# Expert layers of a flow step in passes of 32 slots a head, experts ranked by their count of tokens

## The reference

```python
g_prob = softmax(x @ w_rg + b_rg)                       # 4 groups
g_p, g_i = top_k(g_prob, 1)
e_logits = (x @ w_re + b_re).reshape(-1, 4, 8)
e_v, e_i = top_k(e_logits of group g_i, 2)
gate = softmax(e_v) * g_p
combine = sum(one_hot(g_i * 8 + e_i, 32) * gate)
hid = silu(einsum('nd,edf->nef', x, w_g)) * einsum('nd,edf->nef', x, w_u)
hid = hid * combine
y = hid.reshape(n, 32 * 256) @ w_d.reshape(32 * 256, 1024)
```

## Time and profile before

| | |
|---|---|
| median of 3 runs | 1045.17 us (1044.41 to 1047.46) |
| profiled execution | 1044.07 us |
| its span in the profile | 1042.0 us |
| PE busy | 923.9 us (89%) |
| DVE / ACT / POOL busy | 461.0 / 226.1 / 100.4 us |
| gate and up, L1008 | 229.6 us busy |
| down, L1027 | 116.9 us busy |
| combine, L994 and L995 | 78.6 and 75.6 us busy |
| moved by DMA | 303.99 MB, mean 292 GB/s |
| queue of the weights | 277.08 MB |

### The profile page before, as it was taken

The page is one execution under the profiler, slowest core; times in us unless marked ns, Lnnn a source line. Parts: engine busy times, 40 slices in busy tenths (PEclk is TensorE's granted clock), DMA queues, the critical chain, the costliest instruction groups (busy, mean ns, idle before and its releaser), DMA issues.

```text
span 1042.0 us, 11903 instructions
## 1 busy us (share of the span) xinstructions
PE 923.9 (89%) x4136; PEld 462.2 (44%) x4136; DVE 461.0 (44%) x1037; ACT 226.1 (22%) x458; POOL 100.4 (10%) x164
## 2 busy tenths in 40 slices
PE   2699999999799999999988997899589999999970
PEld 0355454645344444444433465445434444444430
DVE  1257632244323543543555474624515435435454
ACT  2223132212211112112122115212122121111121
POOL 2300011300210000000001000020100000000000
PEclk9899999998799999999998999999689999999995
DMA  9992350948899999999998523021699999999911
GB/s 301 361 351 81 132 184 18 363 167 303 341 398 419 421 420 420 419 422 420 407 372 299 178 81 131 0 87 41 259 418 419 421 420 420 421 420 420 401 50 60
DMA packets 76423, 303.99 MB, mean 292 GB/s; under 512 B 9784, under 2 KB 10096, under 8 KB 50920
## 3 DMA queue, kind: packets, MB, share of 16 engines
q1 hardware_dynamic: 66072, 277.08, 67.2%
q0 software_dynamic: 9040, 21.77, 5.9%
q10 hardware_dynamic: 1280, 4.72, 1.2%
HBM read 310.80 MB, written 5.32 MB: 303 GB/s over the span
## 4 chain that ended last, share of the span: by engine, by line
PE 70%; DMA 14%; DVE 7%; issue 3%; ACT 3%; SPq 2%; POOL 0%; POOLq 0%; DVEq 0%; ACTq 0%
PE psum L1008 18%; PE psum L692 16%; PE psum L1027 8%; DMA ring<-in_w_exp_up 7%; PE psum L764 4%; PE psum L890 4%; PE psum L716 3%; PE psum L980 3%; DVE ht L1767 3%; DMA arena<-h_rows,arena 3%; DMA ring<-in_w_in_odd 2%; DMA ring<-in_w_mod 2%; PE psum L938 1%; PE psum L1131 1%; PE psum L788 1%
## 5 line engine op out<-in xcount | busy, mean ns | idle before, releaser
L1008 PE MATMUL psum<-ring,arena 128*64 128x512 f32 x1024 | 229.6, 601 | 7.4 <-DMA ring<-in_w_exp_up 3.8
L692 PE MATMUL psum<-ring,ht 128*128 128x512 f32 (+1 forms) x432 | 171.9, 555 | 3.4 <-ACT ht L1199 2.7
L1008 PEld LDWEIGHTS psum<-ring,arena 128*64 128x64 f32 x1024 | 82.9, 139 | 151.3 <-issue 151.0
L1027 PE MATMUL psum<-ring,arena 128*64 128x512 f32 x512 | 116.9, 598 | 8.8 <-DVE ht L1767 7.1
L692 PEld LDWEIGHTS psum<-ring,ht 128*128 128x128 f32 x432 | 81.9, 192 | 86.2 <-issue 78.2
L1767 DVE TENSOR_TENSOR ht<-ht,psum 128x512 f32<-128x512 f32 x180 | 110.6, 681 | 4.1 <-PE psum L995 2.2
L1811 DVE TENSOR_TENSOR arena<-arena,psum 128x256 f32<-128x256 f32 x32 | 13.5, 421 | 186.0 <-ACT arena L1342 186.0
L1798 DVE SCALAR_TENSOR_TENSOR y_low<-psum,arena,y_top 128x512 fp32r<-128x512 f32 x64 | 48.0, 751 | 83.6 <-ACT y_top L1349 83.6
L1349 ACT ACTIVATE y_top<-psum,arena 128x512 fp32r<-128x512 f32 x64 | 44.0, 687 | 181.7 <-PE psum L1027 181.7
L994 PE MATMUL psum<-y_top,to_token 128*128 128x512 f32 x192 | 78.6, 409 | 3.5 <-DVE y_low L1798 3.5
L995 PE MATMUL psum<-y_low,to_token 128*128 128x512 f32 x192 | 75.6, 394 | 0.0
(11 more groups left out here) (292 smaller groups left out, 869.4 us busy)
## 6 DMA issues: line engine op xcount, KB each, us to landing
ring<-in_w_exp_gate SPq DMA_DIRECT2D x32, 2048.0 KB, 18.0
ring<-in_w_exp_up SPq DMA_DIRECT2D x32, 2048.0 KB, 22.9
ring<-in_w_exp_down SPq DMA_DIRECT2D x32, 2048.0 KB, 20.5
ring<-in_w_mod SPq DMA_DIRECT2D x24, 2048.0 KB, 18.2
ring<-in_w_in_even SPq DMA_DIRECT2D x5, 2048.0 KB, 19.9
shift_scale<-mod_rows POOLq DMA_DIRECT2D x3, 2048.0 KB, 11.3
ring<-in_w_in_odd SPq DMA_DIRECT2D x3, 2048.0 KB, 21.2
ring<-in_w_out_even SPq DMA_DIRECT2D x2, 2048.0 KB, 8.5
```

Source lines behind the costliest of these rows:

```text
L692: mm = pe.matmul(psum[:, to, 0:cols], HT[:, b, k, :], w[:, k, :], start=(k == 0), stop=(k == KC - 1))
L1008: mm = pe.matmul(psum[64 * e:64 * e + 64, 2, :], XT[:, k, 64 * e:64 * e + 64], RG[:, 3 * v:3 * v + 2, e, k, :], start=(k == 0), stop=(k == ...
L1027: mm = pe.matmul(psum[64 * e:64 * e + 64, 4 + n, :], HTS[v][:, k, 64 * e:64 * e + 64], RD[:, 3 * v + 2, e, k, n * 512:(n + 1) * 512], star ...
```

## The change

1. **Slots.** An expert has 32 slots in a pass (`SLOTS`) instead of 64 in a pair. The array is used in four column groups: gate and up of both experts at once, for which 32 products of 256 columns replace 16 of 512. The down product is cut in the same way: both experts and both halves of the 1024 channels, 8 products of 512 columns in four groups. The result of a pass is one bank: rows 0 to 63 the channels' first half, rows 64 to 127 the second.
2. **Passes.** A round has 22 passes: six heavy places (pairs of experts) with two passes each, then ten light ones with one. An expert of a light place may have 32 tokens, one of a heavy place 64, before a second round is needed.
3. **Rank.** DVE ranks the 32 experts by their count of tokens, the first four experts ahead of all others, since their weights are loaded before the ranks are known. It makes the rank of each token's expert and from this its place; an array `order` gives SP the expert of each rank. SP reads two numbers of it a pair and loads each expert by itself (1 MB a load). A slot is given back by ACT (`gate_up_used`, `down_used`) after the last pass of a pair.
4. **Combine.** Twelve products as before, each over 64 rows only, alternating between rows 0 to 63 and 64 to 127; `to_token` holds the slots twice, so the places' product is made twice. The twelve stand in two parts, before and behind the transposes of `hidden`.
5. **No passes ahead of the loop.** The loop holds all 22 passes; the first one combines zeros. `ACC` is cleared by POOL (a memset of `ht`, 3072 columns) instead of being written by the first pair. Where a semaphore would have been waited for at a value of zero or less, it starts higher.
6. Semaphores of the ring are shared (`first_in_`, `second_in_`).

The core of the diff:

```diff
-HALF = 64
-MAX_ROUNDS = T // HALF
+SLOTS = 32
+HEAVY, LIGHT = 6, 10
+PASSES = 2 * HEAVY + LIGHT
+MAX_ROUNDS = T // (2 * SLOTS)
...
-PLACES = MAX_ROUNDS * PAIRS + 4
+PLACES = MAX_ROUNDS * PASSES + 4
...
+BACK_BANKS = (6, 3, 1, 7, 5, 6)
...
+            def load_experts(l, a, of_pair, slot):
...
+                for e in range(2):
+                    sp.dma_start(RS[:, slot, e:e + 1], w[:, bass.ds(of_pair[e], 1), :]).then_inc(S(f"{('first', 'second')[l]}_in_{slot}"), 16)
...
                 R = rounds_of(sp, l)
+                sp.wait_ge(S("rounds_ready"), 2 * l + 2)
...
+                        place = sp.snap(((i * 2 + u) % PAIRS) * 2)
+                        of_pair = [sp.value_load(order[0:1, bass.ds(place + e, 1)].bitcast(U32), min_val=0, max_val=N_EXP - 1) for e in range(2)]
...
+                        sp.wait_ge(S(f"moe{l}_gate_up_used"), used)
...
+                pool.wait_ge(S("routing_ps"), 4 * l + 1)
+                pool.memset(ht_t[:, :], 0.0).then_inc(S("rows_cleared"), 1)
...
                 pe.wait_ge(S("routing_sb"), 3 * l + 3)
                 for i in range(6):
-                    mm = pe.matmul(psum[:, 7, 0:2 * PLACES], in_slot[:, i, :], in_pair[:, i], start=(i == 0), stop=(i == 5))
+                    for side in range(2):
+                        rows = slice(2 * SLOTS * side, 2 * SLOTS * (side + 1))
+                        mm = pe.matmul(psum[rows, 7, 0:2 * PLACES], in_slot[:, i, :], in_pair[:, i], start=(i == 0), stop=(i == 5))
...
+                def turn_rows(q, v):
+
+                    pe.wait_ge(M(f"gathered_{v}"), (q - v) * 8 + 16)
+                    pe.sem_inc(S("pe_waited"), 1)
+                    for k in range(KC):
+                        t = pe.transpose(psum[:, 0, 2 * SLOTS * k:2 * SLOTS * (k + 1)], XS[v][:, k:D:KC], ident[0:2 * SLOTS, 0:2 * SLOTS])
+                    t.then_inc(M("x_ps"), 1)
+
+                def combine(q, v, blocks):
+
+                    for b in blocks:
+                        for part, rows in enumerate((Y_HI, Y_LO)):
+                            for n in range(2):
+                                if b == NB - 1 and part == 0 and n == 1:
+                                    pe.wait_ge(M("added"), q * 6 + 13)
+                                side = slice(2 * SLOTS * n, 2 * SLOTS * (n + 1))
+                                mm = pe.matmul(bank(BACK_BANKS[2 * b + n]), to_token[v][side, b * P:(b + 1) * P], rows[side, :], start=(part == 0), stop=(part == 1))
...
+                def one_pass(r, p):
+
+                    q = r * PASSES + p
+                    v = p % 2
+                    heavy = p < 2 * HEAVY
+                    place = p // 2 if heavy else p - HEAVY
+                    u = place % 2
+                    new_weights = not heavy or p % 2 == 0
...
                     for k in range(KC):
-                        for e in range(2):
-                            mm = pe.matmul(psum[64 * e:64 * e + 64, 2, :], XT[:, k, 64 * e:64 * e + 64], RG[:, 3 * v:3 * v + 2, e, k, :],
-                                           start=(k == 0), stop=(k == KC - 1))
+                        for a in range(2):
+                            for e in range(2):
+                                to = 2 * SLOTS * (1 - a) + SLOTS * e
+                                mm = pe.matmul(psum[to:to + SLOTS, 2, 0:256], XT[:, k, SLOTS * e:SLOTS * (e + 1)], RG[:, 3 * u + a, e, k, :],
+                                               start=(k == 0), stop=(k == KC - 1))
                     mm.then_inc(M("gate_up"), 1)
+                    turn_rows(q + 1, 1 - v)
+                    if p == 0:
+                        pe.wait_ge(S("table_ready"), 2 * l + 2)
+                        pe.wait_ge(S("rows_cleared"), 7 * l + 7)
+                    results_of(q - 1)
+                    combine(q - 1, 1 - v, range(0, 2))
+                    pe.wait_ge(M("hidden"), q + 3)
...
+                    combine(q - 1, 1 - v, range(2, 3))
+                    pe.wait_ge(M("hidden_t"), q + 1)
...
+                link(dve.scalar_tensor_tensor(key, total, 32.0, key_add, ALU.mult, ALU.add))
...
+                link(dve.tensor_tensor(against, key_other, key_of, ALU.is_gt))
+                link(dve.tensor_reduce(rank, against, AX.X, ALU.add))
...
+                link(dve.tensor_tensor(against, ranked, places_, ALU.is_equal))
+                link(dve.tensor_tensor(against, against, experts_, ALU.mult))
+                link(dve.tensor_reduce(key, against, AX.X, ALU.add))
+                dve.tensor_copy(order.bitcast(U32), key).then_inc(S("rounds_ready"), 1)
```

More of the change, by code:

```diff
@@ L176, in fills_of, with landed_sem @@
 def fills_of(j):
-    return sum(slot_of(i) == slot_of(j) for i in range(j + 1))
+    start = 0 if j < len(FIRST) else len(FIRST)
+    return sum(slot_of(i) == slot_of(j) for i in range(start, j + 1))
+def landed_sem(j):
+    return f"{'first' if j < len(FIRST) else 'second'}_in_{slot_of(j)}"
 def last_in(slot, upto):
@@ L1031, in landed @@
-                def landed(q, v):
-                    return (q - v) * 8 + 16
-                turn_rows(0, 0, first=True)
-                pair(0, 0, first=True)
-                pair(1, 1)
-                R = rounds_of(pe, l)
-                with pe.Fori(1, R * (PAIRS // 2)) as i:
-                    for v in range(2):
-                        pair(i * 2 + v, v)
-                combine(R * PAIRS - 1, 1)
-            experts(0)
+                    if new_weights:
+                        weights_in(2)
@@ new lines, in experts @@
+                start_ = l * len(FIRST)
+                landed = [16 * sum(slot_of(start_ + j) == slot for j in range(len(part_))) for slot in range(RING)]
+                pe.sem_inc(M("back_ps"), 6)
+                pe.sem_inc(M("hidden_ps"), 2)
+                pe.sem_inc(M("down"), 2)
+                pe.wait_ge(S("rest_row_ready"), mods(f"norm_{u}")[0] - FRONT + 1)
+                turn_rows(0, 0)
+                R = rounds_of(pe, l)
+                with pe.Fori(0, R) as r:
+                    for p in range(PASSES):
+                        one_pass(r, p)
@@ L1047, in _ @@
+                last = R * PASSES - 1
+                results_of(last)
+                combine(last, 1, range(0, NB))
+                return last
+            last = experts(0)
             gate, gain = mods("norm_2")
             mod_products(gate)
+            pe.wait_ge(S("moe0_added"), last * 6 + 14)
             mod_sum(gate)
@@ L1354, in experts @@
+                act.sem_inc(M("y_top"), 2)
+                x_copy(0)
                 R = rounds_of(act, l)
-                with act.Fori(1, R * (PAIRS // 2)) as i:
-                    for v in range(2):
-                        pair(i * 2 + v, v)
+                with act.Fori(0, R) as r:
+                    for p in range(PASSES):
+                        one_pass(r, p)
             experts(0)
@@ L1800, in pair @@
[L1800 to L1807 removed]
+                        a = dve.tensor_scalar(to_token[v][:, b * P:(b + 1) * P], iota[:, 0:P], float(b * P), token[v][:, 0:1],
+                                              ALU.add, ALU.is_equal)
@@ L1815, in hidden @@
[L1815 to L1824 removed]
+                    dve.tensor_tensor(HID[v], SGM[v], psum[0:2 * SLOTS, 2, 0:256], ALU.mult).then_inc(M("hidden"), 1)
@@ new lines, in experts @@
+                dve.wait_ge(S("table_ready"), 2 * l + 2)
+                dve.wait_ge(S("rows_cleared"), 7 * (l + 1))
+                dve.sem_inc(M("hidden"), 2)
+                dve.sem_inc(M("y_low"), 2)
+                dve.sem_inc(M("to_token"), 1)
+                dve.sem_inc(M("added"), 6)
+                R = rounds_of(dve, l)
+                with dve.Fori(0, R) as r:
+                    for p in range(PASSES):
+                        one_pass(r, p)
+                last = R * PASSES - 1
```

357 lines of the change are left out of this document (178 added, 179 removed).

## The result

| | before | changed |
|---|---|---|
| median of the runs | 1046.32 us (1044.41 to 1048.54, 4 runs) | **1091.8 us** (1091.36 to 1092.0, 4 runs) |
| span of the profiled execution | 1042.0 | 1089.2 |
| weights' rate, 400 to 500 us | 420 GB/s | 396 GB/s |
| light (before: any) pair in the stream | 15.54 us | 16.64 us |

The change makes the kernel 4.2% slower: ratio 1.042, 95% interval 1.0396 to 1.0444. Forecast were 1067 us and a range of 1044 to 1096.

A forecast was written before the change was run, and what follows sets the result against it. The weight stream was taken to bound the expert layers, PE only 0.5 us a pair behind. Span 1042.0 + 18.3 (layer 1) + 4.1 (layer 2) = 1064.4, giving a forecast of 1067 us, range 1044 to 1096.

The forecast's parts named there:

- A pass: PE in the expert layers: one pass sums to 8.5 us, a light pair taking one and a heavy pair two.
- Short passes: Rival: expert-layer passes take 7.75 us or less but routing delays the stream's start; 1051 us, 20% chance.
- Long passes: Rival: combine's halves don't overlap or register work slows PE, 9.9 us a pass; 1094 us, 16% chance.
- every way to a faster kernel: Rival: passes cost 7.6 us or less and the longer routing stays covered; 1039 us, 11% chance.
- Routing: Each layer's start: DVE's longer chain delays the places' product by 8.8 us; the product takes 5.6.
- The order of the weights on DVE: DVE behind the places' product: making the order takes 4.0 us but ends during pass 0, costing nothing.
- Layer 1's start: Layer 1: pass 2's rows wait for their gather until 309.5 us, so gate_up(2) starts at 314.1.
- the 1.5 us for the stream to start anew: After each layer's last heavy gate product: DMA issue and first bytes may need 1.5 us.
- moves pairs 7 to 15 in 9 x 15.5: Layer 1's light phase: DMA moves the nine remaining pairs in 139.5 us, weights ending at 535.3 against 517.
- I call 15.5 us the stream's price of a pair: Expert layers: the weight stream takes 15.5 us a pair, read from 15.54 us between gate products before the change.
- The lag at layer 2's end: End of layer 2: PE's last down product ends 4.5 us behind the last weights, where it was 17.7.
- loads of one expert run slower: Rival: in the expert layers, split loads drop to 370 GB/s, 17.6 us a pair; 1110 us, 5% chance.

The follow-up runs named there:

- e1: Changed kernel without the row gathers of passes 2 and later, a plain 1 KB copy in place of each: 1060.74 us.
- e16: Kernel before without its row gathers from the third pair on, a plain 1 KB copy in place of each: 1032.33 us.
- e2: Changed kernel with one 2 MB load per pair instead of two of 1 MB, ranked order of the weights left out: 1090.3 us.
- e3: Kernel before with each pair's 2 MB load split into two 1 MB loads back to back: 1044.98 us, ratio 0.999.
- e11: Changed kernel without row gathers of passes 2 and later, and with heavy and light places in turn: 1049.4 us.
- e12: Changed kernel with the comparison of all counts and its sum on DVE done three times in each layer: 1105.75 us.
- e6: Changed kernel with heavy and light places in turn from the third place on: 1092.13 us.
- e15: Changed kernel with gathers alternating between partition halves by pass, and heavy and light places in turn: 1065.49 us, ratio 1.0156 to the kernel before.
- e4: Kernel before with gathers on partitions 0 to 63 alone, tokens of each pair's second expert left out: 1045.24 us.
- e8: Kernel before gathering only the lower 64 rows, issued over 128 partitions with the upper half out of bounds: 1037.45 us, one run.
- e5: Changed kernel with each gather issued over 128 partitions, the upper 64 rows out of bounds: 1082.45 us.
- e13: Changed kernel with gathers over 128 partitions, from pass 2 on the upper 64 fetching the same rows again, unread: 1084.59 us.
- e14: Changed kernel with rows of even passes gathered to partitions 0 to 63, of odd passes to 64 to 127: 1074.31 us.
- e9: Changed kernel with gathered rows at partitions 0 to 31 and 96 to 127, turned by eight float32 products: 1144.8 and 1146.52 us.
- e10: Changed kernel with gathered rows at both ends of the partitions, turned by products, and heavy places spread: 1118.09 and 1119.74 us.

## Why the prediction was right in its sign and wrong in its size

Spans: forecast +22.4, measured 1089.2 - 1042.0 = +47.2.

- **A pass.** Forecast 8.5 us, measured 8.36, in part by luck. Read from the chain of one pass (335.08 to 343.44; forecast in brackets): gate and up 3.45 (3.7), rows 0.91 (0.95), combine 1.96 (1.45), hidden transposes 0.18 (0.25), down 1.85 (1.8), waits nothing (0.35). So combine's halves overlap, but less than forecast, and the waits that were counted once a pass aren't there; the two errors cancel. "Short passes" and "Long passes" both fall, and with the former every way to a faster kernel.
- **Routing.** The places' product was to start 8.8 later and take 5.6; it started 9.85 later and took 4.67, so it ended 10.1 later where 10.0 was said. DVE's part from the first rows' table on grew by 8.2; the other 1.6 lie ahead of it.
- **The order of the weights on DVE** was put at "nothing", and that was wrong. Each layer's first gate product waits for DVE's queue behind it: 2.87 us at 292.91, and in layer 2 4.27 us:

```profile
793.98 5.83 PE L1054 MATMUL psum<-ring,arena 128*32 128x256 f32 x64 [4.27 <-DVEq L1905]
```

ACT had the rows ready 2.1 and 3.6 us earlier. In layer 1 the wait for the gather of pass 2 hides it; in layer 2 nothing does.
- **Layer 1's start.** gate_up(2) at 318.36, forecast 314.1; the gather of pass 2 was waited for, as foretold, until 311.76 instead of 309.5. From there to gate_up(2) it took 6.6 us where 4.6 was said, at a granted clock of 0.57 in 310 to 318. The last heavy gate product ended at 397.05, forecast 394.3: +2.8. The stream's idle time in the heavy phase, forecast 1.5 us a pair, is seen only without gathers: the DMA share of 310 to 400 us is 0.89 in e1 and 0.96 in the changed kernel. No run shows the 1.5 us for the stream to start anew.
- **The step that failed** is "moves pairs 7 to 15 in 9 x 15.5", that is, "I call 15.5 us the stream's price of a pair", carried over to the changed kernel. That price had two parts, 14.93 of weights and 0.6 of gathered rows (e1, e16), and the change nearly tripled the second, to 1.7. In layer 1 the way from the last heavy gate product to w_in_odd's landing took 7.3 us more than forecast. In layer 2 the last heavy gate product ended at 891.8 where the forecast, moved by the 27.2 us with which layer 2 begins later, said 892.0 (an agreement that owes something to luck: the wait for DVE is made up by an earlier places' product and shorter passes). The last down product ended at 1051.3 instead of 1037.5: +13.8. Nine pairs at 1.1 us more are 9.9; the other 3.9 weren't taken apart, and the late engines at the end are a likely part.
- **The lag at layer 2's end.** Forecast were 4.5 us between the last weights and the last down product; the rate reached nothing at about 1046, and the product ended 5 us later, at 1049.33 + 1.92. PE does what was expected of it, the weights are late:

```profile
1041.28 5.07 PE L1054 MATMUL psum<-ring,arena 128*32 128x256 f32 x64 [4.80 <-issue]
...
1049.33 1.92 PE L1076 MATMUL psum<-ring,arena 128*32 128x512 f32 x16
```

- **The sum.** 18.3 + 2.8 + 7.3 in layer 1, -1.1 between the layers, 4.1 + 13.8 in layer 2, 2.1 behind it: 47.3.
- **Rival "loads of one expert run slower".** Its symptom came in a weaker form (376 to 408 GB/s against its 370), its cause did not: e2 and e3 exclude it. Had I read the symptom alone, I would have named the wrong part. The gather was on my list only as a latency ("No gather is late" in layer 2, true) and as POOL's queue, never as bytes in the stream that fall on some engines.
- Read by the runs, the 45.5 us are 16.0 for gathers (31.1 in the changed kernel less the 15.1 that the kernel before paid too), 11.3 for heavy pairs that stand together, and 18.2 for all the rest. Without gathers and with heavy pairs spread, e11 is still 17.1 above e16. By e12, which passes on all that DVE does longer, the rest is mainly the longer routing of two layers, against the shorter tail; it wasn't measured apart.

## What to carry to other kernels

A period read from a trace is a sum; before it is carried over a change, take it apart by what the change touches. Here 6.29 MB at 420 GB/s is 15.0, not 15.5, and asking for the missing 0.5 would have led to the gathers. Where small transfers run beside a saturated stream, price them by the engine that gets most of them, and spread their rows over all partitions: 47 rows over both halves cost 0.6 us, 38 in one half 1.4. A DMA share of 1.0 does not say that pairs land at the mean rate; look at how the stream ends, where engines that are behind show as a long, thin tail. And a reordering (e6) can be worth nothing until another cost is gone (e15). Count, before a second pass is built in, how often it has work.

## What the runs showed of the hardware that was not expected

- **The price of gathered rows went by the partitions that they are written to, not by their number in all.** 24 rows in each half cost 0.6 us a pair (kernel before), 24 in one half 0.7 (e4, e8), 38 in one half, 19 from partition 0 and 19 from 32 on, 1.4 (e5); doubling them into the other half nothing (e13), alternating halves 0.6 (e14). So the halves have DMA engines of their own. The Trainium skill (SBUF — State Buffer, Door 1: The DMA port swizzle) says that a partition's port follows from bits 2 to 4 and bit 6 of its number, so that 32 further is the same port and 64 further another. By that the fullest port gets 8 rows of 4 KB a pair in e5 and 4 in the kernel before, e4 and e8; the runs agree: double the rows on a port, about double the price (1.4 against 0.6 to 0.7). And 19 rows from partition 0 on, with 19 more from 32 on, reach 5 of 16 ports; the tail of e5, with 2 to 4 tenths of the engines at work, agrees. An estimate from the runs: one of 16 engines at 420 GB/s in all moves 4 rows in 0.6 us and 8 in 1.2. That rows 32 apart share a path is not shown by itself: no run moved rows by 32 partitions alone.
- A gather issued over 64 partitions also makes the weights' rate dip to 325 to 369 GB/s (e4), and the same rows issued over 128 do not (e8). It cost the changed kernel about 0.3 us a pair (16.64 against 16.37). Why is open.
- Turning 64 rows by eight float32 products with a slice of the identity took 4.0 to 4.1 us (e9; 4.01 in e10), by eight transposes 0.9 (changed kernel).
